# First attention of a two-block transformer kernel: its score products regrouped as 128, 128 and 32 contracted rows

## The reference

```python
q_nope, q_rope = q[..., :64], apply_rope(q[..., 64:], cos, sin)   # 8 heads
k_nope, v = kv[..., :64], kv[..., 64:]
k_rope = apply_rope(u_kr, cos, sin)                               # one for all heads
s = einsum("bqhd,bkhd->bhqk", q_nope, k_nope) + einsum("bqhd,bkd->bhqk", q_rope, k_rope)
p = softmax(s * 96 ** -0.5)
o = einsum("bhqk,bkhd->bqhd", p, v)
```

## Time and profile before

| | |
|---|---|
| median of 3 runs | 2779.03 us (2778.56 to 2780.07) |
| the profiled execution | 2780.26 us, span 2778.3 us |
| busy: TensorE, its weight loads | 98%, 82% of the span |
| busy: VectorE, ScalarE, GpSimd | 65%, 45%, 16% |
| DMA | 137 GB/s on average |

### The profile page before, as it was taken

How to read it: one execution, slowest core, us unless ns; L and a number is a source line. 1 busy time by engine, 2 the same in 40 slices (tenths; PEclk the granted TensorE clock), 3 DMA queues, 4 the chain that set the end, 5 groups by cost and what they waited for, 6 DMA issues and landing times.

```text
span 2778.3 us, 36356 instructions
## 1 busy us (share of the span) xinstructions
PE 2726.2 (98%) x14436; PEld 2281.4 (82%) x14436; DVE 1800.1 (65%) x2497; ACT 1259.2 (45%) x2026; POOL 439.2 (16%) x393
## 2 busy tenths in 40 slices
PE   8999999999999999999999999999999999999998
PEld 7978888788884888888888887878888868888898
DVE  3646888330546888888885968988886572110575
ACT  4333787141432777777776124454454453111101
POOL 1500231000011211111102000000001043221341
PEclk9999999999999999999999999999999999999999
DMA  4041000420217999999982121030121221110141
GB/s 140 31 154 46 31 1 1 165 93 32 92 67 294 391 396 396 396 396 396 395 326 69 61 104 49 20 118 28 60 72 42 94 76 46 46 46 31 60 145 61
DMA packets 141604, 379.79 MB, mean 137 GB/s; under 512 B 11952, under 2 KB 45234, under 8 KB 141309
## 3 DMA queue, kind: packets, MB, share of 16 engines
q1 hardware_dynamic: 126140, 325.22, 30.9%
q0 software_dynamic: 12560, 42.74, 4.9%
q10 hardware_dynamic: 2736, 9.50, 0.9%
HBM read 341.13 MB, written 35.26 MB: 135 GB/s over the span
## 4 chain that ended last, share of the span: by engine, by line
PE 91%; DVE 4%; ACT 2%; DMA 1%; issue 1%; POOL 0%; SPq 0%; ACTq 0%; POOLq 0%; DVEq 0%
PE ps L2988 8%; PE ps L2989 8%; PE ps L2990 8%; PE ps L2591 7%; PE ps L2973 6%; PE ps L2975 6%; PE ps L2974 6%; PE ps L3082 3%; PE ps L3084 3%; PE ps L3083 3%; PE ps L2605 3%; PE ps L3129 2%; PE ps L3094 1%; PE ps L3096 1%; PE ps L3095 1%; PE ps L3114 1%
## 5 line engine op out<-in xcount | busy, mean ns | idle before, releaser
L2310 DVE SCALAR_TENSOR_TENSOR b_f<-b_f,small_f 128x1023 f32<-128x1023 f32 (+14 forms) x240 | 304.3, 1268 | 27.0 <-ACT small_f L1279 13.8
L2988 PE MATMUL ps<-x_f32r,w_f32r 128*128 128x512 f32 x480 | 187.9, 392 | 4.3 <-DVE b_f L2507 3.6
L2990 PE MATMUL ps<-x_f32r,w_f32r 128*128 128x512 f32 x480 | 187.4, 390 | 0.0
L2974 PE MATMUL ps<-w_f32r,a_f32r 128*128 128x512 f32 x456 | 177.4, 389 | 0.0
L2989 PE MATMUL ps<-ht_f32r,w_f32r 128*128 128x512 f32 x416 | 162.5, 391 | 0.0
L3083 PE MATMUL ps<-w_f32r,a_f32r 128*128 128x512 f32 x384 | 149.9, 390 | 0.0
L2974 PE MATMUL ps<-x_f32r,a_f32r 128*128 128x512 f32 x312 | 121.4, 389 | 0.0
L1279 ACT ACTIVATE x_f<-ps 128x512 f32<-128x512 f32 (+1 forms) x184 | 91.0, 533 | 44.4 <-PE ps L2591 21.0
L1209 POOL TENSOR_TENSOR w_f32r<-w_f,w_f32r 128x2048 fp32r<-128x2048 f32 x23 | 110.2, 4793 | 1.9
L2988 PEld LDWEIGHTS ps<-x_f32r,w_f32r 128*128 128x128 f32 x480 | 90.4, 188 | 23.7 <-issue 4.9
L2990 PEld LDWEIGHTS ps<-x_f32r,w_f32r 128*128 128x128 f32 x480 | 90.5, 189 | 18.9
(11 more groups left out here) (578 smaller groups left out, 7870.6 us busy)
## 6 DMA issues: line engine op xcount, KB each, us to landing
w_f<-in_w_exp_up SPq DMA_DIRECT2D x40, 1024.0 KB, 10.3
w_f<-in_w_exp_down SPq DMA_DIRECT2D x38, 1024.0 KB, 10.2
w_f<-in_w_exp_gate SPq DMA_DIRECT2D x36, 1024.0 KB, 8.8
...
```

The lines of the kernel that those rows point to most:

```text
L2310: ins = v.scalar_tensor_tensor(C_conv[k][:, d:S], U_conv[k][:, 0:S - d], cols[:, k, R_TAP + j:R_TAP + j + 1], C_conv[k][:, d:S], ALU.mult, ...
L2974: mm(o, x1, w2[:, k, c], start=False, stop=False)
L2988: mm(o, l1, r1, start=(k == 0), stop=False)
L2990: ins = mm(o, l2, r1, start=False, stop=(k == n - 1))
```

## The change

The three products of a half, 96 rows each, are regrouped so that both high and low parts stand side by side on the partitions:

- first, 128 rows: `q_hi`, which now has the plain high part twice, with `k_both`, where rows 0 to 63 are the keys' low part and 64 to 127 their high part;
- second, 128 rows: `q_rest` (plain low part; the rotated high part in rows 64 to 95 and again in 96 to 127) with `k_hi` (plain high part; the rotated key's high part, then its low part);
- third, 32 rows: `r_lo` (the rotated query's low part) with `s_hi` (the rotated key's high part). It is placed in row group 0 or 2 for the first half of the keys and 1 or 3 for the second, by the parity of the head.

Each is issued for both halves before the next. The low-by-low product of the rotated features stays out as before. To feed this, ScalarE rounds each head's plain part twice (`head_hi`, two instructions) and the rotated queries of all heads once (`rope_round`), VectorE makes the low parts of these and of the rotated key, GpSimd copies the rotated key into its places, 14 copies of 32x512, and SyncE moves 64 pieces of 16x1024 (8 for the first head, 28, a wait for all of them, 28). TensorE gets three waits: for GpSimd and `q_first` ahead of step 0, for `q_rest` ahead of step 8.

```diff
--- before.py
+++ after.py
@@ -613,11 +613,15 @@
         ang = mem(GB0 + 2176, NF)
         ang2 = mem(GB0 + 2176 + NF, NF)
         pq = mem(HT0, 8192).rearrange("p (c r m k) -> p c r m k", c=4, r=8, m=2)
-        KT = mem(HT0, 8192)[0:HD1, :].rearrange("p (h s) -> p h s", h=H1)
-        QT = mem(GA0, 8192)[0:HD1, :].rearrange("p (h s) -> p h s", h=H1)
-        KT_lo = mem_r(HT0, 8192)[0:HD1, :].rearrange("p (h s) -> p h s", h=H1)
-        QT_lo = mem_r(GA0, 8192)[0:HD1, :].rearrange("p (h s) -> p h s", h=H1)
-        k_hi, q_hi = ([mem_r(GC0 + at_ + 1024 * i, 1024)[0:HD1, :] for i in range(2)] for at_ in (0, 2048))
+
+
+        KT, QT = (mem(at_, 8192)[0:NOPE, :].rearrange("p (h s) -> p h s", h=H1) for at_ in (HT0, GA0))
+        k_both, q_rest = (mem_r(at_, 8192).rearrange("p (h s) -> p h s", h=H1) for at_ in (HT0, GA0))
+        k_hi, q_hi = ([mem_r(GC0 + at_ + 1024 * i, 1024) for i in range(2)] for at_ in (0, 2048))
+        s_hi = mem_r(HN_AT + 1024, 1024)
+        s_lo = mem_r(SPARE, 1024)[0:ROPE, :]
+        rope_hi, rope_lo = ([mem_r(at_ + 1024 * m, 1024) for m in range(2)] for at_ in (SPARE, up_slot["kvup"]))
+        r_lo = [mem_r(at_, 1024) for at_ in (up_slot["kvup"] + 2048, up_slot["kvup"] + 3072, SPARE, SPARE + 1024)]
         Vr = mem_r(X0, 8192).rearrange("p (t h m d) -> p t h m d", t=T, h=H1, m=2)
         V_all = mem_r(X0, 8192).rearrange("p (t h d) -> p t h d", t=T, h=H1)
         pt_hi, pt_lo = ([mem_r(GB0 + 4096 * i + at_, 2048).rearrange("p (k q) -> p k q", k=8) for i in range(2)] for at_ in (0, 2048))
@@ -813,8 +817,8 @@
         def head_parts(nm, h):
 
             if nm == "k":
-                return KT[:, h, :], k_hi[h % 2], KT_lo[:, h, :]
-            return QT[:, h, :], q_hi[h % 2], QT_lo[:, h, :]
+                return KT[:, h, :], (k_hi[h % 2][0:NOPE, :], k_both[NOPE:P, h, :]), k_both[0:NOPE, h, :]
+            return QT[:, h, :], (q_hi[h % 2][0:NOPE, :], q_hi[h % 2][NOPE:P, :]), q_rest[0:NOPE, h, :]
 
         def whole_parts(name):
 
@@ -925,14 +929,25 @@
                     for t in range(T):
                         bk.read(sp, ("y1f", t, 0)), bk.read(sp, ("y1f", t, 1))
                         sp.dma_start(dram["x1"][tile(t), :], X[:, t, :]).then_inc(sem(f"x_tile{t}"), 16)
-                    for j in range(2):
-                        c = slice(NB * j, NB * j + NB)
-                        sp.wait_ge(sem("q_rope"), j + 1)
+                    sp.wait_ge(sem("q_rope"), 4)
+
+                    def upper(h, name):
                         for m in range(2):
-                            sp.dma_start(QT[NOPE + 16 * m:NOPE + 16 * m + 16, 0, c], rope_out[m][0:16, c]).then_inc(sem(f"q_first{j}"), 16)
+                            for r in (NOPE, NOPE + ROPE):
+                                sp.dma_start(value(q_rest[r + 16 * m:r + 16 * m + 16, h, :]), value(rope_hi[m][16 * h:16 * h + 16, :])).then_inc(sem(name), 16)
+
+                    def lower(h, name):
+                        for m in range(2):
+                            for r in (NOPE * (h % 2), NOPE * (h % 2) + ROPE):
+                                sp.dma_start(value(r_lo[h // 2][r + 16 * m:r + 16 * m + 16, :]), value(rope_lo[m][16 * h:16 * h + 16, :])).then_inc(sem(name), 16)
+
+                    upper(0, "q_first"), lower(0, "q_first")
                     for h in range(1, H1):
-                        for m in range(2):
-                            sp.dma_start(QT[NOPE + 16 * m:NOPE + 16 * m + 16, h, :], rope_out[m][16 * h:16 * h + 16, :]).then_inc(sem("q_rest"), 16)
+                        upper(h, "q_rest")
+                    sp.wait_ge(sem("q_first"), 16 * 8)
+                    sp.wait_ge(sem("q_rest"), 16 * 4 * (H1 - 1))
+                    for h in range(1, H1):
+                        lower(h, "q_rest")
                     bk.wait(sp, ("s1", 2 * T - 1))
                     for i in range(2):
                         sp.dma_start(mem(WO_AT[2 * i], 2048).rearrange("p (k n) -> p k n", k=2), w_mix[1][:, 2 * i:2 * i + 2, :]).then_inc(sem("wo_in"), 16)
@@ -1087,10 +1102,16 @@
                 one = tab[:, 0:16 * T].rearrange("p (t f) -> p t f", f=16).unsqueeze(2).to_broadcast([P, T, H1, 16])
                 nc.gpsimd.tensor_copy(wide, one).then_inc(sem("tables"), 1)
             pool.wait_ge(sem("tables"), 3)
+            bk.wait(pool, ("vt", T - 1))
             for j in range(2):
                 c = slice(NB * j, NB * j + NB)
                 bk.read(pool, ("kr", j))
-                nc.gpsimd.tensor_copy(KT[NOPE:HD1, 1:H1, c], KT[NOPE:HD1, 0:1, c].to_broadcast([ROPE, H1 - 1, NB])).then_inc(sem("k_rope"), 1)
+                for r in range(ROPE, P, ROPE):
+                    nc.gpsimd.tensor_copy(s_hi[r:r + ROPE, c], value(s_hi[0:ROPE, c]))
+                for i in range(2):
+                    nc.gpsimd.tensor_copy(k_hi[i][NOPE:HD1, c], value(s_hi[0:ROPE, c]))
+                    ins = nc.gpsimd.tensor_copy(k_hi[i][HD1:P, c], value(s_lo[:, c]))
+                ins.then_inc(sem("k_rope"), 1)
 
 
             for i in range(NS):
@@ -1098,7 +1119,7 @@
                 if h + 1 < H1 and t in (3, 5):
                     pool.wait_ge(sem("head_hi"), 2 * (h + 1) + (t - 3) // 2 + 2)
                     whole, hi, lo = head_parts("kq"[(t - 3) // 2], h + 1)
-                    nc.gpsimd.tensor_tensor(lo, whole, value(hi), ALU.subtract).then_inc(sem("head_lo"), 1)
+                    nc.gpsimd.tensor_tensor(lo, whole, value(hi[0]), ALU.subtract).then_inc(sem("head_lo"), 1)
                 if i >= 35 and i % 2 and i <= 41:
                     k = (i - 35) // 2
                     pool.wait_ge(sem("out_hi"), 4 + k + 1)
@@ -1386,21 +1407,34 @@
 
             def head_hi(nm, h, c=slice(0, S)):
                 whole, hi, lo = head_parts(nm, h)
-                nc.scalar.activation(hi[:, c], whole[:, c], ACT.Copy).then_inc(sem("head_hi"), 1)
+                nc.scalar.activation(hi[1][:, c], whole[:, c], ACT.Copy)
+                nc.scalar.activation(hi[0][:, c], whole[:, c], ACT.Copy).then_inc(sem("head_hi"), 1)
 
             bk.read(act, ("kf", 0, 0)), bk.read(act, ("kf", 0, 1))
             bk.read(act, ("kr", 0)), bk.read(act, ("kr", 1))
             head_hi("k", 0)
+
+            def rope_round(h):
+                act.wait_ge(sem("k_rope"), 2)
+                act.wait_ge(sem("q_rope"), h + 1)
+                for m in range(2):
+                    ins = nc.scalar.activation(rope_hi[m][:, NB * h:NB * h + NB], rope_out[m][:, NB * h:NB * h + NB], ACT.Copy)
+                ins.then_inc(sem("rope_hi"), 1)
+
+            rope_round(0)
             for c, h in QF[:4]:
                 heads_copy(("qf", c, h), QT, c, h, HD1 ** -0.5)
+                if (c, h) == (0, 0):
+                    rope_round(1)
             bk.read(act, ("qf", 0, 0)), bk.read(act, ("qf", 0, 1))
             for j in range(2):
-                act.wait_ge(sem(f"q_first{j}"), 32)
                 head_hi("q", 0, slice(NB * j, NB * j + NB))
             nc.scalar.activation(rsum[:, NS - 1:NS], half[:, 0:1], ACT.Exp)
 
             def mix_round(c):
                 bk.read(act, ("o1", 8 * c + 7))
+                if c == 0:
+                    act.wait_ge(sem("q_rest"), 16 * 8 * (H1 - 1))
                 nc.scalar.activation(mixa_hi[:, c, :], mixa[:, c, :], ACT.Copy).then_inc(sem("mix_hi"), 1)
 
             for i in range(-1, NS + 2):
@@ -1415,8 +1449,6 @@
                 if 0 <= i < NS:
                     m = i // 2
                     if i == 1:
-                        act.wait_ge(sem("k_rope"), 2)
-                        act.wait_ge(sem("q_rest"), 16 * 2 * (H1 - 1))
                         for c, u in KF:
                             bk.read(act, ("kf", c, u))
                         for c, u in QF:
@@ -2003,7 +2035,7 @@
             def head_low(nm, n, c=slice(0, S)):
                 dve.wait_ge(sem("head_hi"), n)
                 whole, hi, lo = head_parts(nm, 0)
-                v.tensor_tensor(lo[:, c], whole[:, c], value(hi)[:, c], ALU.subtract).then_inc(sem("block1_lo"), 1)
+                v.tensor_tensor(lo[:, c], whole[:, c], value(hi[0])[:, c], ALU.subtract).then_inc(sem("block1_lo"), 1)
 
             for c, h in KF:
                 if c % 2:
@@ -2015,8 +2047,11 @@
                     for k in ((0, 1), (2,))[c // 2]:
                         up_rest(qn_r[:, k, :], qn[:, k, :], qn_hi[:, k, :])
             for j in range(2):
+                c = slice(NB * j, NB * j + NB)
+                bk.wait(dve, ("rt", 1, 1))
                 b = bk.wait(dve, ("kr", j))
-                bk.done(v.tensor_copy(KT[NOPE:HD1, 0, NB * j:NB * j + NB], PS[0:ROPE, b, :]), ("kr", j))
+                ch(v.tensor_copy(s_hi[0:ROPE, c], PS[0:ROPE, b, :]))
+                bk.done(v.tensor_tensor(s_lo[:, c], PS[0:ROPE, b, :], value(s_hi[0:ROPE, c]), ALU.subtract), ("kr", j))
             for t in range(T):
                 dve.wait_ge(sem("psum_hi"), XH + 8 + t + 1)
                 b = bk.at[("vt", t)][0]
@@ -2038,6 +2073,12 @@
```

(23 more changed lines are left out.)

## The result

The changed kernel takes 2816.6 us (median of 4 runs, 2816.29 to 2818.09), the kernel before 2779.4 on the same chip (2778.56 to 2780.07): 1.0135 times as long [1.0118, 1.0153], some 37 us slower. The forecast was 2806 with a range of 2796 to 2815. The direction and the places were right, the size was 10 us short, and the time lies just outside the range.

What follows compares the result with a forecast made beforehand. TensorE, busy for 98% of the span, was taken to bound the kernel. Terms of 13.2 + 3.1 + 2.6 + 5.4 + 2.9 = 27.2 us on 2779.0 gave 2806.2, say 2806 us, range 2796 to 2815.

Steps and rivals of the forecast that it cites:

- part 2: SyncE's 64 transfers of the rotated queries: TensorE waits for them ahead of the ninth score product, +13.2 us.
- Part 3: TensorE's granted clock falls to half after its standstill at the ninth product, +2.6 us, between 1.7 and 3.4.
- Part 1: Score products on TensorE: changing the array's shape costs more than pairing the 32-row products saves, +3.1 us over 28 pairs.
- first rival: TensorE's score products: the 32-row pair switches shape free, so 28 pairs save 6.4 us; 2799 us; chance 0.12.
- Part 4: ScalarE's second rounding of q delays GpSimd and TensorE at the ends of six heads, 0.9 us each, +5.4 us.
- Part 5: ScalarE is full at i = 18, 34, 50 and 36, where extra roundings make TensorE wait, +2.9 us together.
- third rival: SyncE's queue: on-chip transfers issue fast, so not slower; 2791 us alone, chance 0.03; with the first rival 2783, 0.03.

Runs made afterwards that it cites:

- e1: The change without VectorE's wait for `k_rope` ahead of the first head's low part of k: 2811.5 us, 1.0109 of the kernel before.
- e2: The change with heads 1 to 3 transferred first, upper and lower, the others waited for only at product 32: 2804.3 us, 1.0085 of the kernel before.
- e3: The change with both 32-row products of a step in one row group instead of two: 2828.4 us, 1.0171 of the kernel before.
- e8: The change with VectorE's wait dropped, transfers by head, second rounding later; 32-row pair replaced by repeated 128-row products: 2789.1 us, 1.0033 of the kernel before.
- e9: The change with VectorE's wait dropped, transfers by head, second rounding later; 32-row pair ahead of the full products: 2792.9 us, 1.0043 of the kernel before.
- e10: The change with VectorE's wait dropped, transfers by head, second rounding later; 32-row pair issued twice: 2807.9 us, 1.0099 of the kernel before.
- e5: The change with ScalarE first rounding the copy GpSimd waits for, TensorE waiting separately for the second: 2810.4 us, 1.0106 of the kernel before.

## Why the prediction was wrong in size, and right in kind

**Where it failed: the start of the chain in part 2.** "VectorE ends the rotation of the second half at 258.98": that kept VectorE's timing of before and overlooked two things. VectorE waits for `k_rope` ahead of the first head's low part of k, a line that the diff doesn't show because it didn't change; what changed was what stands behind that semaphore, two copies before, now 14. And the price of those copies, 0.46 each by columns from the earlier trace rows (the row gives 0.45), "done by 253 to 254": they took 0.61 us at a pitch of 0.655, from 246.92 to 256.05. Their number alone is not to blame: in the kernel before the copies began at 236.22, in the change they also wait for the last `vt` product. VectorE has both halves of the rotated key ready at 238.6, so 14 copies begun then would have ended by about 248 (an estimate from the pitch), before VectorE asks; that was not run. The prediction had asked whether these copies were "in time" for TensorE and ScalarE, and never who else waits for them. The rotation then ended at 265.25, 6.3 us later than forecast; product 0 came at 274.89 instead of 268.3, product 8 at 312.94 instead of 305.4. That is 7.5 of the 10 us. e1 shows the wait to be the cause of most of it: of 6.3 us at SyncE's first transfer (267.86 against 261.6), 4.7 come back without it, 5.4 when the 0.63 us are taken off by which that execution was late ahead of the edit. The rest is that the copies then slow VectorE down beside them (1.07 us in three instructions), which the prediction didn't have either.

**Part 2 otherwise** held: pitch 0.63 to 0.64, landing 2.3 to 2.4, and between products 0 and 8 it said 37.1 us and 38.05 passed. Its mechanism, that TensorE waits at product 8 for the queue, e2 shows.

**Part 3, the clock**: forecast 2.6 us for the wait at product 8; the step behind it took 7.39 instead of 4.42, 3.0 us. The loss is right and the stretches are not: a low clock of 3 to 7 us was expected, and there were two, of 10.2 and 13.7 us, the first behind the wait at product 0. TensorE stood still in part of each.

**Part 1, the products**: forecast +0.11 for two steps, measured +0.15, 4.4 us instead of 3.1 (what is left of the 16.35 between products 8 and 63 when the terms below are taken off). The extra of 0.32 was taken between two groups of other shapes; it is 0.29 up to the transposes and 0.06 on the next one, a share the prediction named ("before what that transpose loses itself") and didn't count. e3, e8, e9 and e10 bear the mechanism out: pairs at the pitch of one (e3, e10), a price once a group (e10) that outweighs the pitch saved (e8) and stays with the pair (e9). The first rival, that the pair switches free, fell: with full rows in its place (e8) two steps are 0.14 shorter. The Trainium skill's "TensorE: Matmul & The Clock Gate", The mechanism, has such tiles start about 4 ns apart; the trace agrees with 3 ns. But the start of the pair isn't where the time goes.

**Part 4, the second rounding of q**: forecast 6 x 0.9, measured 6 x 1.09 with the pair's 0.11 in it, 5.9 us; e5 shows it. **Part 5, ScalarE full**: forecast 2.9, measured 1.09 + 1.20 + 1.09 less 0.11 each, 3.05 us. Parts 1 and 3 to 5 together were forecast at 14.0, the stage from product 8 to 63 grew by 16.35.

**Behind the stage** nothing was forecast and the trace has 1.0 us more (2298.4 from product 63 to the end, before 2297.5). The runs made here change nothing there and show 2294.9 (e2) to 2299.3 us (e1), so it says nothing about the change.

**The range**: its ends were given as parts 2 to 4 at their bounds, 2797 to 2813. The bounds as written (10 to 15 us, 1.7 to 3.4, 6 x 0.5 to 6 x 1.1) add up to 2800 to 2810; none of them held a wait of VectorE for GpSimd.

The third rival (transfers that issue fast) fell with the first row of SyncE's queue.
